# A hybrid SSM decoder step on one core: 16 modulation tiles moved into the SSD stage, sample states loaded by SyncE, mixer norms gathered

## Chip, cores and metric

One Trainium2 chip, one core. The metric is the device time of one execution in microseconds. Before the change the median of three runs is 2753.36 us (2751.09 to 2754.26).

## The reference

One decoder layer works on 256 prompt tokens and 8 sample tokens (one step for each of 8 sequences that carry states), D = 2048. A conditioning vector per sequence gives 6 x 2048 modulation values (`mod = silu(c) @ w_ada + b_ada`). The mixer has two halves, an SSD half (16 heads of 64) and a gated delta (GDN) half (8 heads of 128 x 128 state):

```
mod = silu(c) @ w_ada + b_ada
sh1, sc1, g1, sh2, sc2, g2 = split(mod, 6)
hm = rmsnorm(x, norm1_w) * (1 + sc1) + sh1
z, xbc, dt_raw, qkv, a_raw, b_raw, gate = split(hm @ w_in)
y = ssd_scan(conv(xbc), ...) ;  y = rmsnorm(y * silu(z), in 2 groups of 512)
o = gdn_scan(conv(qkv), ...) ;  o = rmsnorm(o, per head of 128) * silu(gate)
x = x + g1 * (concat(y, o) @ w_out)
hf = rmsnorm(x, norm2_w) * (1 + sc2) + sh2
x = x + g2 * peer(hf)        # product keys, top 16 of 128^2 experts
y_out = rmsnorm(x, final_norm_w)
```

For a sample token the GDN recurrence is one step: S is scaled by exp(g), k and q are multiplied with it, and beta k (v - S^T k)^T is added. The new states are outputs.

## The kernel before

Everything is float32; large products split weights and activations into a high and a low part and take three products of them. 264 columns are the 256 prompt tokens and 8 sample tokens. Weights come as tiles of 1 MB through a ring of four slots (`wring`), loaded by SyncE (SP) in one fixed order (lines 388 to 416): 32 w_ada tiles, 52 of w_in, 64 of w_ada (`N_ADA2`), 16 of w_out, 16 of w_q, then the experts. A slot is loaded again when `gemm_done` or `lo_ready` says that it has been used, so the order of the queue is the order of use.

Stages in order of time:

1. Modulation, first 32 tiles. One tile is 4 matmuls of 512 columns on TensorE (`ada_part`, L475); after four tiles ScalarE (ACT) copies bank 6 to `adasb` (L911, L1035, L1059) and four small matmuls turn it into columns of bank 7 (`ada_turn`), counted by the semaphore `ada_ps`. VectorE (DVE) later adds the bias into `mod`.
2. w_in with convolution and gates, to about 464 us.
3. SSD stage (TensorE L533 to L594), to about 525 us. GpSimd (POOL) writes decay rows to DRAM and loads them back broadcast to 128 partitions (`BR`, L1893, 4 MB). DVE builds decays, POOL the weighted x (L1902 to L1905), TensorE the first state (`h1_ps`), the final state (`hf_ps`), and y in two chunks (L574) and from the carried state (L586). No weight tile is used here; the next four w_ada tiles have landed before it.
4. GDN loop (L608), four passes of two heads, to about 726 us. Each pass has 12 w_ada tiles between the steps of its triangular inverse (`ada(i, j)`, L597). POOL updates the SSD states of two samples in each pass.
5. The tail, from `gdn_free` 5 (L690) to the first w_out tile (L718). TensorE's program is: `ada_rest(0)`; `norm(4)` twice (y, two groups of 4 tiles); the product for q.k; 64 small products of the sample states with k and q (`gst`, 128x128 by 2 columns), with `ada_rest(1)` in their middle; a transpose; four norms of one head and `ada_rest(2)`; four more and `ada_rest(3)`. POOL loads the eight pieces of `gst` (L1971, 512 KB each, in runs of 512 B) after its loop, and after the products scales both halves of them (L1977, recorded under L1876), which DVE waits for before `mixl` (L1579). A norm is: squares (ACT L877), a product with ones, root (ACT L886), reciprocal (DVE L1253), and scaling (DVE L1246). At its end ACT makes `mixh` and DVE `mixl`, the high and low parts of the concatenated y and o (L1079 to L1084).
6. w_out, 16 tiles. Per tile DVE makes the low part of the next tile's weights, adds the result to x, and adds k v^T to four sample states (L1611); POOL loads `gvb` for 16 states at a time (L1984) and stores the new states (L1989).
7. Norm, w_q, expert retrieval and experts, to the end.

Of the kernel before, what the change touches and what calls it, by code (L numbers as in the profile page):

```python
# [73 lines left out]
T_REST = T_ADA2 + 48  # L74
# [36 lines left out]
def build(nc, a, o):  # L111
    with ExitStack() as ctx:
# [132 lines left out]
        h1h, h1h_f = take_r(KT, T)  # L245
        mixh = view(zg_off, KT, T, of=F32R)
# [38 lines left out]
        vn, ksm, vsm = take(64), take(64), take(64)  # L285
        vrow = take(128, parts=64)
# [70 lines left out]
        def _(sp):  # L357
# [35 lines left out]
            four(a["w_out"], gemm_done, T_OUT)  # L393
            tiles(a["w_out"], lo_ready, L_OUT, N_OUT, first=1)
# [35 lines left out]
        def _(pe):  # L430
# [101 lines left out]

            pe.wait_ge(sem("zg_ready"), N_GATE + SLOTS)  # L533
            pe.wait_ge(sem("cv_ready"), 2 * CT + 8)
            for c in range(2):
                for j in range(8):
                    tr(ps[:, 2 * c + j // 4, (j % 4) * 128:(j % 4 + 1) * 128], cv[:, TX + j, c * CH:(c + 1) * CH]
                       ).then_inc(sem("xt_ps"), 1)
            pe.wait_ge(sem("cs_ready"), 1)
            for c in range(2):  # L540
                for g in range(2):
                    last = tr(ps[:, 7, (2 * c + g) * 128:(2 * c + g + 1) * 128], cv[:, TB + g, c * CH:(c + 1) * CH])
            last.then_inc(sem("bt_ps"), 1)
# [11 lines left out]
            last.then_inc(sem("h1_ps"), 1)  # L555

# [34 lines left out]

            pe.wait_ge(sem("y_evac"), 24)
# [4 lines left out]
            def ada(i, j):  # L597

                s, n = j % SLOTS, j // SLOTS
                pe.wait_ge(landed[s], i * 48 + (T_ADA2 // SLOTS * 16 + 16 * n + 16))  # L600
                if s == 0 and n:
                    ada_turn(i * 3 + (N_ADA1 // SLOTS + n), (n - 1) * (SLOTS * NC))
# [5 lines left out]
            with pe.Fori(0, 4) as i:  # L608
# [48 lines left out]
                ada_turn(i * 3 + (N_ADA1 // SLOTS + 3), 2 * SLOTS * NC)  # L657
# [26 lines left out]
            def ada_rest(g):  # L684
                for s in range(SLOTS):
                    pe.wait_ge(landed[s], 16 * (T_REST // SLOTS + g + 1))
                    ada_part(s)
                ada_turn((T_REST - T_ADA2 + N_ADA1) // SLOTS + g + 1, g * SLOTS * NC)

            pe.wait_ge(sem("gdn_free"), 5)  # L690
# [1399 lines left out]
```

## Time and profile before

| | us |
|---|---|
| median of three runs | 2753.36 |
| profiled execution | 2749.44 |
| its span, first to last instruction | 2747.9 |
| PE matmuls busy | 2487.0 (91%) |
| DVE busy | 1902.9 (69%) |
| ACT busy | 1003.3 (37%) |
| POOL busy | 484.8 (18%) |
| mean granted TensorE clock | 0.954 |

PE is TensorE's matmuls and PEld its weight loads, which overlap them. The profile is that of the profiled execution, 1.5 us shorter in its span than in its own device time. Busy shares are averages over stages with different limits. A clock of 1.00 is 2.4 GHz and 0.50 is 1.2 GHz. Most TensorE instructions carry the helper's line L437 (`mm`), and those of DVE L1240 (`tt`) or L1246 (`stt`), so they are told apart by time and shape. One float32 matmul is recorded as two instructions. In a timeline row of several instructions the duration runs from the first's start to the last's end.

### The profile page before, as it was taken

The page shows a single profiled execution, that of the slowest core. Times are in us where ns is not written, and L with a number is a line of the kernel's source. Part 1 is how long each engine was busy: PE and PEld are TensorE (multiplying, and loading weights), DVE is VectorE, ACT ScalarE, POOL GpSimd, SP SyncE. Part 2 cuts the span into 40 slices and gives each one's busy share as a digit, 9 for nine tenths or more (in the row PEclk, how much of TensorE's full clock was granted, in tenths as well). Part 3 has the DMA queues.
Part 4 walks back from the last instruction along what each step waited for, and adds up shares of the span by engine and source line. Part 5 has one row for each costly group of instructions (what it writes and reads, how often), then busy time and mean ns, then how long its engine had stood idle before and what let it go on. Part 6 is the DMA issues. An engine that isn't in the chain of part 4 may idle for free.

```text
span 2747.9 us, 54567 instructions
## 1 busy us (share of the span) xinstructions
PE 2487.0 (91%) x21637; PEld 2330.8 (85%) x21637; DVE 1902.9 (69%) x2496; ACT 1003.3 (37%) x1173; POOL 484.8 (18%) x221
## 2 busy tenths in 40 slices
PE   6489998687668799999899999999999999999998
PEld 2189997455448689899899999999999999999997
DVE  0377765534337678988999878778778778666666
ACT  1156686111113332144343333333334333333333
POOL 0000000455420110046333212112112121000000
PEclk8799999799869899999999999999999999999999
DMA  8545544387836733344344444454444444555553
GB/s 363 243 155 182 183 165 172 134 320 261 306 135 245 249 138 138 138 154 154 123 153 148 159 171 168 163 176 154 170 170 165 174 166 160 182 183 178 174 182 124
DMA packets 71422, 500.01 MB, mean 182 GB/s; under 512 B 8132, under 2 KB 8396, under 8 KB 14320
## 3 DMA queue, kind: packets, MB, share of 16 engines
q1 hardware_dynamic: 64368, 465.38, 46.7%
q0 software_dynamic: 6912, 32.50, 3.5%
q8 instruction: 117, 1.92, 0.3%
q14 instruction: 25, 0.20, 0.0%
HBM read 483.51 MB, written 14.35 MB: 181 GB/s over the span
## 4 chain that ended last, share of the span: by engine, by line
PE 81%; DVE 9%; DMA 4%; issue 4%; ACT 1%; POOL 1%; DVEq 0%; SPq 0%; ACTq 0%; POOLq 0%
PE ps L437 78%; DVE sb L1240 7%; DMA sb<-in_w_ada 3%; PE ps L475 2%; DVE sb L1246 1%; DVE sb L1243 1%; DMA sb<-rows_dram 0%; POOL sb L1876 0%; POOL sb L1971 0%; DMA sb<-in_state_gdn 0%; DVE sb L1253 0%; DMA out_gdn_state_s<-sb 0%; PE ps L574 0%; DVEq L1240 0%; ACT sb L936 0%
## 5 line engine op out<-in xcount | busy, mean ns | idle before, releaser
L437 PEld LDWEIGHTS ps<-sb,sb 128*128 128x128 f32 (+1 forms) x20680 | 2290.7, 176 | 285.3 <-issue 156.8
L437 PE MATMUL ps<-sb,sb 128*128 128x264 f32 (+5 forms) x20680 | 2352.2, 274 | 184.3 <-DVE sb L1240 94.2
L1240 DVE TENSOR_TENSOR sb<-sb,sb 128x264 fp32r<-128x264 f32 (+13 forms) x988 | 1321.7, 1372 | 370.3 <-ACT sb L936 250.7
L936 ACT CAST sb<-sb 128x2048 fp32r<-128x2048 f32 x327 | 624.8, 1911 | 566.7 <-PE ps L437 559.5
L1876 POOL TENSOR_TENSOR sb<-sb,sb 128x1056 bf16<-128x1056 bf16 (+3 forms) x158 | 439.6, 2789 | 1124.8 <-DVE sb L1240 1057.5
L1240 DVE TENSOR_TENSOR sb<-sb,ps 128x264 f32<-128x264 f32 (+2 forms) x577 | 248.6, 449 | 120.3 <-PE ps L437 100.0
L1205 ACT ACTIVATE sb<-ps 128x264 f32<-128x264 f32 x96 | 37.5, 391 | 359.0 <-PE ps L437 359.0
L475 PE MATMUL ps<-sb,sb 128*32 128x512 f32 x768 | 117.8, 710 | 34.1 <-DMA sb<-in_w_ada 22.8
L1240 DVE TENSOR_TENSOR sb<-ps,sb 128x256 f32<-128x256 f32 (+6 forms) x45 | 13.5, 327 | 159.2 <-PE ps L437 153.7
L1246 DVE SCALAR_TENSOR_TENSOR sb<-sb,sb,sb 128x288 f32<-128x288 f32 (+3 forms) x220 | 95.3, 462 | 21.8 <-DMA sb<-v_dram 3.9
L1122 ACT COPY sb<-ps 128x352 f32 (+1 forms) x96 | 82.4, 870 | 28.4 <-PE ps L437 28.3
L475 PEld LDWEIGHTS ps<-sb,sb 128*32 128x32 f32 x768 | 18.6, 119 | 83.7 <-DMA sb<-in_w_ada 53.1
L1886 POOL DMA_DIRECT2D rows_dram<-sb x1 | 0.7, 705 | 467.1 <-DVE sb L1364 467.1
L1150 ACT ACTIVATE sb<-ps 128x264 f32<-128x264 f32 x32 | 12.5, 390 | 153.3 <-PE ps L437 153.3
L1243 DVE TENSOR_SCALAR sb<-sb,sb 128x288 f32<-128x288 f32 (+2 forms) x69 | 24.8, 388 | 49.4 <-ACT sb L957 49.1
L1041 ACT COPY sb<-ps 128x512 f32<-128x512 f32 x24 | 14.1, 586 | 102.2 <-PE ps L437 102.2
L1246 DVE SCALAR_TENSOR_TENSOR sb<-ps,sb,sb 128x256 f32 (+1 forms) x24 | 10.2, 438 | 44.1 <-PE ps L437 44.1
L911 ACT COPY sb<-ps 128x512 f32<-128x512 f32 x8 | 4.7, 585 | 82.5 <-PE ps L475 82.5
L955 ACT COPY sb<-ps 128x256 f32<-128x256 f32 x36 | 13.5, 374 | 54.1 <-PE ps L437 54.1
L1348 DVE RECIPROCAL sb<-sb 128x264 f32<-128x264 f32 x16 | 28.7, 1797 | 5.8 <-ACT sb L980 5.8
L1253 DVE RECIPROCAL sb<-sb 128x264 f32<-128x264 f32 x13 | 23.4, 1799 | 11.5 <-ACT sb L886 11.4
L877 ACT ACTIVATE sb<-sb 128x264 f32<-128x264 f32 x64 | 24.7, 418 | 17.5 <-PE ps L437 10.9
(128 smaller groups left out, 500.3 us busy)
## 6 DMA issues: line engine op xcount, KB each, us to landing
sb<-in_peer_u SPq DMA_DIRECT2D x128, 1024.0 KB, 4.8
sb<-in_peer_v SPq DMA_DIRECT2D x128, 1024.0 KB, 4.7
sb<-in_w_ada SPq DMA_DIRECT2D x96, 1024.0 KB, 7.7
sb<-in_w_in SPq DMA_DIRECT2D x52, 1024.0 KB, 4.8
sb<-in_w_out SPq DMA_DIRECT2D x16, 1024.0 KB, 4.9
sb<-in_w_q SPq DMA_DIRECT2D x16, 1024.0 KB, 4.7
sb<-rows_dram POOLq DMA_DIRECT2D x1, 4096.0 KB, 11.9
sb<-in_state_ssd POOLq DMA_DIRECT2D x8, 512.0 KB, 5.5
```

Of the source, the lines that this page charges most:

```text
L437: return pe.matmul(out, l, r, start=start, stop=stop)
L475: last = pe.matmul(ps[32 * j:32 * j + 32, 6, :], sT[:, 4 * s + j, :], wring[:, s, :, :].rearrange("p (k c) n -> p k (c n)", k=4)[:, j, :], ...
L877: act.activation(sqb[:, n % 4, :], src, ACT.Square).then_inc(sem("sq_ready"), 1)
L936: act.copy(whi[:, slot % 2], wring[:, slot]).then_inc(sem("hi_ready"), 1)
L1122: act.copy(G[:, bass.ds(quarter, QE), bass.ds(t0, GT)].rearrange("p a t -> p t a"), ps[:, bank + b, 0:GT * QE].rearrange("p (t a) -> p t a ...
L1205: act.activation(craw[:, s % 2, :], ps[:, s % 2, 0:T], ACT.Gelu).then_inc(sem("gelu_done"), 1)
L1240: return dve.tensor_tensor(out, x, y, op)
L1243: return dve.tensor_scalar(out, x, s1, s2, op0, op1)
L1246: return dve.scalar_tensor_tensor(out=out, in0=x, scalar=s, in1=y, op0=op0, op1=op1)
L1253: link(dve.reciprocal(nrm[:, k % 2, :], nrm[:, k % 2, :]))
L1348: link(dve.reciprocal(r, r))
L1876: return pool.tensor_tensor(out, x, y, op)
```

## The change

- TensorE gets four groups of four w_ada tiles in the SSD stage: after the x transposes, after `h1_ps`, after `hf_ps`, and between the two y chunks. The loop of stage 4 then takes tiles 16 to 63 of the 64, and nothing is left for the tail. ACT copies these groups in `ada_early`; DVE adds `mod` of the 16 tiles ahead of the loop. Banks in the SSD stage are changed so that banks 6 and 7 are free.
- SyncE loads the sample states behind the first four w_out tiles: `gst1` after `gdn_free` 5, `gst0` after the last stores of `S2` and of the SSD states.
- The prompt columns of both mixers are normed together: 16 squares, 16 matmuls with a selecting weight of 32 columns into one bank of 32 rows, one root, one reciprocal of 32 rows; ten matmuls with a column of the identity spread each row to 128 partitions, and DVE scales from PSUM.
- The sample columns of o are normed apart, after the state products, 64 columns at once; `mixh` and `mixl` are made in three pieces.
- The states are scaled by DVE, four at a time, in the w_out loop, no longer by POOL.

The core of the diff:

```diff
-T_REST = T_ADA2 + 48
+N_SSD = 16
+T_GDN = T_ADA2 + N_SSD
...
             four(a["w_out"], gemm_done, T_OUT)
+            sp.wait_ge(sem("gdn_free"), 5)
+            for h in (4, 5, 6, 7):
+                sp.dma_start(gst1[:, 8 * (h % 4):8 * (h % 4) + 8, :], gdn_s_in[:, h]).then_inc(sem("ld_gst1"), 16)
+            for c in range(2):
+                sp.wait_ge(sem(f"sst_stored{c}"), 64)
+            sp.wait_ge(sem("s2_stored"), 64)
+            for h in range(4):
+                sp.dma_start(gst0[:, 8 * h:8 * h + 8, :], gdn_s_in[:, h]).then_inc(sem("ld_gst"), 16)
             tiles(a["w_out"], lo_ready, L_OUT, N_OUT, first=1)
...
+            def ada_tiles(g):
+                for s in range(SLOTS):
+                    pe.wait_ge(landed[s], T_ADA2 // SLOTS * 16 + 16 * g + 16)
+                    ada_part(s)
...
+            ada_tiles(0)
+            pe.wait_ge(sem("norm_sqrt"), 17)
             pe.wait_ge(sem("cs_ready"), 1)
...
             last.then_inc(sem("h1_ps"), 1)
+            ada_turn(A_SSD + 1, 0)
+            ada_tiles(1)
...
             last.then_inc(sem("hf_ps"), 1)
-            pe.wait_ge(sem("norm_sqrt"), 17)
+            ada_turn(A_SSD + 2, SLOTS * NC)
+            ada_tiles(2)
             pe.wait_ge(sem("h1_ready"), 1)
             for c in range(2):
                 pe.wait_ge(sem("m_ready"), c + 1)
                 if c == 1:
+                    ada_turn(A_SSD + 3, 2 * SLOTS * NC)
+                    ada_tiles(3)
                     pe.wait_ge(sem("y_evac"), 8)
...
+            ada_turn(A_SSD + 4, 3 * SLOTS * NC)
             pe.wait_ge(sem("y_evac"), 24)
...
             pe.wait_ge(sem("gdn_free"), 5)
-            ada_rest(0)
-            norm(4)
-            norm(4)
+            for j in range(2 * HG):
+                n = sq_n[0]
+                sq_n[0] += 1
+                row = j if j < HG else HG + (j - HG) // 4
+                pick = (row_o if j < HG else row_y)[:, 31 - row:63 - row]
+                pe.wait_ge(sem("sq_ready"), n + 1)
+                mm(ps[0:32, 4, 0:T], pick, sqb[:, n % 4, :], j == 0, j == 2 * HG - 1).then_inc(sem("sq_used"), 1)
...
+            pe.wait_ge(sem("ld_gst1"), 64)
+            state_products(range(32, 48))
+            pe.wait_ge(sem("rows_ready"), 1)
+            for j in range(2 + HG):
+                row = HG + j if j < 2 else j - 2
+                n = T if j < 2 else TP
+                bank, at = (5 + j, 0) if j < 2 else ((7, 0, 3, 4)[row // 2], row % 2 * TP)
+                mm(ps[:, bank, at:at + n], ident[0:32, row:row + 1].broadcast_to([32, P]), nrm[0:32, k17 % 2, 0:n]
+                   ).then_inc(sem("row_ps"), 1)
+            state_products(range(48, 64))
+            pe.wait_ge(sem("ld_gst"), 64)
+            state_products(range(32)).then_inc(sem("skq_ps"), 1)
             pe.wait_ge(sem("vns_ready"), 1)
-            for half in range(2):
-                for h in range(4):
-                    norm(1)
-                ada_rest(2 + half)
-            pe.wait_ge(sem("mixl_ready"), 2)
+            mm(ps[:, 6, 0:64], ones, sqb[:, n % 4, 0:64]).then_inc(sem("sq_used"), 1)
+            pe.wait_ge(sem("mixl_ready"), 3)
...
+            dve.reciprocal(rows, rows).then_inc(sem("rows_ready"), 1)
             for g in range(2):
-                r = inv_root()
+                dve.wait_ge(sem("row_ps"), g + 1)
                 for j in range(4):
                     t = 4 * g + j
+                    st.mark(stt(cv[:, TX + t, :], cv[:, TX + t, :], ynw[:, t:t + 1], ps[:, 5 + g, 0:T],
+                                ALU.mult, ALU.mult))
...
+            for h in range(HG):
+                dve.wait_ge(sem("row_ps"), h // 2 * 2 + 4)
+                v, at = cv[:, TQ + h, 0:TP], h % 2 * TP
+                st.mark(stt(v, v, onw[:, 0:1], ps[:, (7, 0, 3, 4)[h // 2], at:at + TP], ALU.mult, ALU.mult))
...
-            dve.wait_ge(sem("gst_scaled"), 2)
...
                         tt(xT[:, n, TP:T], xT[:, n, TP:T], gtmp[:, s, :], ALU.add).then_inc(sem("x1_done"), 1)
+                        four = gst[half][:, bass.ds(i * 16 + 4 * s, 4), :]
+                        link(tt(four, four, over(egc[:, bass.ds(i * 16 + (32 * half + 4 * s), 4)], 128, 2), ALU.mult))
...
-            for h in range(8):
-                pool.dma_start(gst[h // 4][:, 8 * (h % 4):8 * (h % 4) + 8, :], gdn_s_in[:, h]
-                               ).then_inc(sem("ld_gst"), 16)
-            pool.wait_ge(sem("skq_ps"), 1)
-            for j in range(2):
-                s4 = gst[j].rearrange("p (h b) v -> p h b v", b=TS)
-                tt(s4, s4, over(SR[:, 16 + 4 * j:20 + 4 * j, 0, :], 128, 3), ALU.mult).then_inc(sem("gst_scaled"), 1)
```

## Rows read from the trace of the kernel before

**Rows 1.** Stages: us, busy (count) per engine, PE clock, DMA share, GB/s
```profile
483.00:525.00 42.00, 18.92 (x136) 15.00 (x136) 26.74 (x47) 10.26 (x13) 10.20 (x5) 0.66 0.05 14
...
677.00:726.00 49.00, 42.17 (x320) 29.24 (x324) 17.91 (x33) 7.32 (x14) 29.31 (x20) 0.96 0.82 313
...
738.00:763.00 25.00, 0.00 (x0) 0.00 (x0) 4.26 (x8) 0.26 (x1) 4.40 (x5) 0.59 0.67 206
```

**Rows 2.** Timeline of the tail: start us, us, engine, instruction, count, [idle before]
```profile
725.88 5.21 PE L475 MATMUL ps<-sb,sb 128*32 128x512 f32 x32 [2.58 <-DVE sb L1246]
...
735.16 1.35 ACT L877 ACTIVATE sb<-sb 128x264 f32<-128x264 f32 x4
...
735.30 1.80 DVE L1253 RECIPROCAL sb<-sb 128x264 f32<-128x264 f32 x1 [5.60 <-ACT sb L886]
...
735.72 2.19 PE L437 MATMUL ps<-sb,sb 128*128 128x264 f32 x10 [0.97 <-ACT sb L877]
...
737.13 1.71 DVE L1246 SCALAR_TENSOR_TENSOR sb<-sb,sb,sb 128x264 f32<-128x264 f32 x4
...
748.39 2.64 POOL L1971 DMA_DIRECT2D sb<-in_state_gdn  x3 [15.94 <-issue]
...
763.72 13.78 PE L437 MATMUL ps<-sb,sb 128*128 128x2 f32 x64 [25.81 <-DMA sb<-in_state_gdn]
...
783.18 11.96 PE L437 MATMUL ps<-sb,sb 128*128 128x9 f32 x72 [0.71 <-ACT sb L1059]
...
795.23 14.01 POOL L1876 TENSOR_TENSOR sb<-sb,sb 128x4096 f32<-128x4096 f32 x2 [36.45 <-PE ps L437]
...
795.43 13.89 DVE L1240 TENSOR_TENSOR sb<-sb,sb 128x64 f32<-128x64 f32 x2
...
814.79 3.64 PE L475 MATMUL ps<-sb,sb 128*32 128x512 f32 x32
...
830.70 2.36 DVE L1240 TENSOR_TENSOR sb<-sb,sb 128x2112 f32<-128x2112 f32 x1
...
838.50 31.73 PE L437 MATMUL ps<-sb,sb 128*128 128x264 f32 x246 [5.06 <-DVE sb L1240]
```

**Rows 3.** Columns as rows 1, two microseconds within the products
```profile
789.00:791.00 2.00, 2.00 (x11) 2.00 (x11) 0.00 (x0) 0.00 (x0) 0.00 (x0) 0.50 1.01 426
```

**Rows 4.** DMA view, 748 to 757 us: rate in 40 slices; us to landing
```profile
GB/s 0 0 0 0 0 0 0 0 55 255 91 73 36 237 510 346 309 291 291 273 310 309 291 291 291 291 273 291 291 291 291 291 291 219 164 37 0 0 0 0
...
sb<-in_state_gdn POOLq DMA_DIRECT2D x3, 512.0 KB, 5.8
```

**Rows 5.** DMA view, first GDN pass, 525 to 576 us: rate in slices
```profile
GB/s 13 0 55 315 305 305 350 392 353 212 366 411 424 424 424 411 341 389 437 414 424 418 411 430 276 238 392 270 405 389 382 411 382 350 373 77 0 0 0 42
```

**Rows 6.** DMA view, 464 to 484 us: the broadcast, us to landing
```profile
sb<-rows_dram POOLq DMA_DIRECT2D x1, 4096.0 KB, 11.9
```

**Rows 7.** Timeline of the SSD stage, TensorE, columns as rows 2
```profile
485.90 3.75 PE L437 MATMUL ps<-sb,sb 128*128 128x512 f32 x4 [14.71 <-POOL sb L1876]
...
492.64 5.46 PE L437 MATMUL ps<-sb,sb 128*128 128x128 f32 x32 [2.98 <-POOL sb L1876]
...
498.03 1.97 PE L574 MATMUL ps<-sb,sb 128*64 128x128 f32 x32
...
509.31 3.68 PE L574 MATMUL ps<-sb,sb 128*64 128x128 f32 x32 [9.31 <-DVE sb L1240]
```

**Rows 8.** DMA view, 735 to 748 us, queues: packets, MB, share
```profile
q1 hardware_dynamic: 317, 2.22, 47.7%
q0 software_dynamic: 396, 1.43, 30.6%
```

**Rows 9.** DMA view, 473 to 476 us, within the broadcast
```profile
q0 software_dynamic: 32, 1.05, 83.4%
```

**Rows 10.** Groups by shape, 464 to 940 us: busy, mean ns, idle
```profile
L1240 DVE TENSOR_TENSOR sb<-sb,sb 128x512 f32<-128x512 f32 x12 | 12.4, 1029 | 3.5 <-ACT sb L1029 2.8 <-DVE sb L1240 0.2
```

**Rows 11.** Waits, 839 to 935 us: us in total, times, longest
```profile
DVE sb L1246 <- PE ps L437: 22.2, 15, 3.2
```

More of the change, by code:

```diff
@@ L245, in build @@
         h1h, h1h_f = take_r(KT, T)
+        row_y, row_o = take(64), take(64)
         mixh = view(zg_off, KT, T, of=F32R)
@@ L285, in build @@
         vn, ksm, vsm = take(64), take(64), take(64)
+        egc, bec = take(64), take(64)
         vrow = take(128, parts=64)
@@ L681, in _ @@
                 last.then_inc(sem("s_ps"), 1)
[L684 to L688, printed above, removed]
-            pe.wait_ge(sem("gdn_free"), 5)
-            ada_rest(0)
-            norm(4)
-            norm(4)
+            pe.wait_ge(sem("gdn_free"), 5)
+            for j in range(2 * HG):
[5 more added lines that the diff above has]
+                mm(ps[0:32, 4, 0:T], pick, sqb[:, n % 4, :], j == 0, j == 2 * HG - 1).then_inc(sem("sq_used"), 1)
+            k17 = norms[0]
+            norms[0] += 1
             pe.wait_ge(sem("qkp_ready"), 1)
@@ L1081, in _ @@
             act.wait_ge(sem("mix_ready"), 2)
-            act.copy(mixh[:, 8:16], cv[:, TQ:TQ + 8, :]).then_inc(sem("mixh_ready"), 1)
+            act.copy(mixh[:, 8:16, 0:TP], cv[:, TQ:TQ + 8, 0:TP]).then_inc(sem("mixh_ready"), 1)
+            high(0, T_OUT // SLOTS * 16 + 16, None)
+            act.wait_ge(sem("vrow_ps"), 1)
+            act.copy(vrow, ps[0:64, 5, 0:128]).then_inc(sem("vrow_ready"), 1)
+            act.wait_ge(sem("o_ready"), 1)
+            n, k18 = sq_n[0], norms[0]
+            sq_n[0] += 1
+            norms[0] += 1
+            act.wait_ge(sem("sq_used"), n - 3)
+            act.activation(sqb[:, n % 4, 0:64].rearrange("p (h b) -> p h b", b=TS), cv[:, TQ:TQ + 8, TP:T], ACT.Square
+                           ).then_inc(sem("sq_ready"), 1)
+            act.wait_ge(sem("sq_used"), n + 1)
+            act.activation(nrm[:, k18 % 2, 0:64], ps[:, 6, 0:64], ACT.Sqrt, scale=1.0 / P, bias=epsc[:, 0:1]
+                           ).then_inc(sem("norm_sqrt"), 1)
+            act.wait_ge(sem("mix_ready"), 3)
+            act.copy(mixh[:, 8:16, TP:T], cv[:, TQ:TQ + 8, TP:T]).then_inc(sem("mixh_ready"), 1)
             def high_next(i, s, t0):
@@ L1434, in _ @@
             dve.sem_inc(sem("ysm_ready"), 1)
+            dve.wait_ge(sem("ada_ps"), A_GDN)
+            link(tt(mod[:, 32:48, :], ps[:, 7, 0:16 * NC].rearrange("p (n c) -> p n c", c=NC),
+                    over(bada[:, 32:48], NC, 2), ALU.add))
             dve.wait_ge(sem("norm_free"), 17)
```

143 lines of the change are left out of this document (78 added, 65 removed).

## The prediction

> **What bounds the kernel now.** I read the busy time by stage first [rows 1]. The gated-delta loop (GDN) keeps TensorE (PE) busy 42 us of 49. Between that loop and w_out it does not: for 25 us it does nothing at all (738 to 763). The SSD stage is thin as well: behind the broadcast of the decay rows PE works 18.9 of 42 us while the DMAs move 14 GB/s. These two places are what the change touches. Then the timeline of the tail [rows 2]: the GDN loop lets PE go at 725.88 (call it G), and the first w_out matmul starts at 838.50, G+112.6. Between them lie, one after another, 16 modulation tiles in four groups; sample states that come so late that the products start at 763.72; 64 head products around one of the groups; a sample update on DVE, two instructions that are held for 13.89 us while POOL scales the states; eight norms with a reciprocal of 1.80 us each; two copies and two subtractions of 128x2112. Then the granted clock [rows 3], the DMAs [rows 4 to 6] and the SSD stage [rows 7], whose PE waits 14.71 us for the broadcast.
>
> **The tail, part by part.** All times are from G.
> Norm sums: 16 matmuls of 264 columns. At full clock one costs 0.44 us (10 matmul instructions in 2.19 us, two per matmul) [rows 2]. PE comes out of the loop slow: its first 32 modulation matmuls took 5.21 us, against 3.64 for 32 at 814.79 [rows 2]. That is 1.6 us lost, so some 3.3 us at half clock, and 3.3 + 12.2 x 0.44 = 8.7 us. The squares on ACT, 0.34 each (1.35 for 4) [rows 2], are faster than that and hide beside PE; without that cover they would be 16 x 0.34 = 5.4. One root (0.5), then one reciprocal, still 1.80 though it has 32 rows, since the row at 735.30 pays for its 264 columns: rows ready at G+11.2.
> States: SyncE issues gst1's four loads at G and gst0's about 3 us later, when the last gdn_p store has landed; the w_out tiles that stand before them in its queue land during the last GDN pass. POOL's loads, alone, moved some 291 GB/s [rows 4]: 2.1 MB in 7.2 us, seen about 2 us later, gst1 at G+9.7 and all at G+17.5. POOL's issue stall of 15.94 us [rows 2] goes with the queue. No row shows SyncE loading pieces of 512 B. From below, the 424 GB/s of weight tiles [rows 5]: all at G+12. From above, one behind another at the 5.8 us landing of POOL's loads: gst1 at G+23, all at G+46. I take POOL's rate, the same pieces on the same DMAs.
> Products: 16 of them fill the wait for the rows, 32 instructions x 0.107 = 3.4 us, G+13.3. Ten row matmuls of 256 to 264 columns, 4.4 us, G+17.7. 48 products are left, 96 instructions. Before, 64 instructions took 13.78 us, 0.215 each, half clock; the 72 at 783.18 took 11.96, which is a mixture, and PE stood at 0.50 from 789 to 791 though it was busy without a gap [rows 2, 3]. If x of the 72 ran at 0.107 and the rest at 0.215, 11.96 us gives x = 33, some 3.6 us. I count 4 us at full clock (37 instructions) and 59 instructions at 0.215, 12.7 us: G+34.4.
> Here the Trainium skill says otherwise. "TensorE: Matmul & The Clock Gate", What's actually happening, has the gate set by how busy PE has been, so that unbroken products should hold the full clock. By that rule they would end at G+28. The trace does not agree: busy 2.00 of 2.00 us, clock 0.50 [rows 3].
> DVE: 8 y and 8 o scalings at 0.43 to 0.49 us (1.71 for 4), the gate and one half of mixl at 2.36 each [rows 2] end at G+26.8, and ACT's copies and first high part at G+28.3: both inside the products, which are their cover.
> Behind the products: six small updates 1.6, mixl of the prompt 2.3, reciprocal of 64 columns 0.45 (an estimate, 1.80 x 64/264), scaling, gate, copy and subtraction 1.3: 5.7 us. The first w_out matmul at G+40.1. **Tail 112.6 to 40.1: -72.5.** Late next is PE itself.
>
> **What it costs elsewhere.** SSD stage. A group of four tiles is 3.6 to 5.2 us of PE [rows 2], plus a turn of 1 to 1.9. Group 0 (landed long before) lies in the 14.71 us wait: nothing. But it frees its slots from 470 on, so 4.2 MB of weights start beside the 4.2 MB broadcast that lands 11.9 us after its issue [rows 6]. Where two queues shared, that with 8 KB packets had 47.7% and that with 4 KB packets 30.6% [rows 8], so shares go by packet. The broadcast's packets are 32 KB [rows 9]; an 8 KB packet between any two of them adds a quarter of its 10 us: +3 (ends: 0, weights wait behind it; +10, even bytes). Group 1 sits between the first-state and the final-state product: h1 ends at 492.7, turn and tiles take until 498.5, where the operands are there at 495.6. Group 2 waits for its tiles: slots free from 495.4, four tiles at 424 GB/s [rows 5] take 9.9 us and 2 to be seen, 507.5. PE reaches the y product at 508.7, before at 498.03 [rows 7]: +10.7. Group 3 is hidden: its last tile lands at about 517 and is done at 518.3, and the next operand comes 11.3 us after the y product (509.31 - 498.03), at 520. With PE busy before it, the block that took 3.68 us for the instructions that took 1.97 at 498.03 [rows 7] runs partly at full clock, and the next too: -1.5. One addition of mod is new before the loop: 0.3. **SSD +9.5**, ends +4 and +20 (no landing hidden).
> GDN loop: 12 tiles a pass as before, the first four landed before it starts: 0.
> w_out: DVE gets 16 scalings of 128x512, taken at 0.7 us; the nearest group of that size has 1.03 in the mean, POOL beside it [rows 10]. DVE waits 22.2 us for PE in 15 tiles, 1.5 each [rows 11], so this is hidden; without the cover 11 to 16 us. Only the last one lies on the path, before the last state store: +0.8.
> **Sum: -72.5 + 9.5 + 0.8 = -62.** The profiled execution took 2749.44 (span 2747.9 and 1.5 around it), so 2687. The median of the three runs is 2753.36, 3.9 above it: I say 2691.
>
> **Rivals.**
> 1. Even sharing. The weights take half of the DMAs from the broadcast: it lands at +10 instead of +3, SSD +16, in sum 2697. The packets of 8 and 32 KB speak against [rows 8, 9]. The Trainium skill, "DMA: Bandwidth & Descriptors", SWDGE vs HWDGE vs iDMA, gives a packet as preferably at most 4096 B and as the boundary at which an engine changes queues; by that rule the shares would be even. Chance 0.15.
> 2. The clock holds in the products, as norm and row matmuls stand around them: -6.3, 2685. The 13.78 us at half clock speak against [rows 2]. 0.12.
> 3. Late states. With half of the upper bound's lateness gst0 lands at G+32, the 32 products on it take 13.8 us, w_out starts at G+51.5: 2702. At the bound, G+46: 2716. POOL's issue stall can have been its own queue's, which speaks against. 0.13.
> 4. The modulation part does nothing: only the 26 us of waiting for states and POOL's 14 go, and SSD's +10 stays: 2723. Rows of 5.21 and 3.64 us for its groups in the chain speak against [rows 2]. 0.03.
> 5. Slower. DVE bounds w_out, since each scaling, which is on DVE now, is held as the two updates were (6.9 us each) [rows 2]. 16 x (6.9 - 1.5) = 86, in sum +24: 2777. It decides from 1.5 + 62/16 = 5.4 us a scaling. For it: both read two SBUF operands. Against: POOL only issues DMAs in this stretch. 0.02.
>
> **How the numbers follow.** My case has 0.55, the rivals 0.15, 0.12, 0.13, 0.03 and 0.02. The range takes in its bounds (SSD +4 and +20), rivals 1 and 2 whole and most of 3: 2676 to 2712. A measurement of this kernel can tell about 0.2%, 5.5 us, from no change. Faster by more: 0.96. Within: 0.02. Slower by more: 0.02.
>
> **What would show it.** Right: no POOL tensor_tensor of 4096 and no held update; products at clock 1.0 and then 0.50; first w_out matmul 40 us after the GDN loop; the loop starting 9.5 us later, rows_dram landing in 15 us; PE waiting for in_w_ada once in the SSD stage, before the y product; DVE still waiting for PE in w_out. Wrong: PE waiting for in_state_gdn past G+18; rows_dram over 20 us; a GDN loop more than 2 us longer; PE waiting for DVE in w_out.

## The result, and the profile after

The changed kernel takes 2732.9 us (median of 7 executions, 2720.5 to 2738.4), the kernel before, on the same chip, 2751.7. The ratio is 0.9927, 95% interval 0.9905 to 0.9949: faster by some 20 us, where the forecast was 62 and its range ended at 2712. The profiled execution of the changed kernel took 2735.1 us with a span of 2733.5.

To see where the other 42 us went, each kernel was profiled four times (the first two profiles and runs e1, e5, e12 to e15 below); before: the first, e5, e12, e14; after: the first, e1, e13, e15. The stages, cut at TensorE's (PE's) first matmul in each, means of four in us:

| stage | before | after | difference | forecast |
|---|---|---|---|---|
| start to first GDN matmul (SSD stage) | 525.5 | 549.6 | +24.1 | +9.5 |
| GDN loop | 202.1 (200.8 to 204.4) | 209.4 (207.6 to 211.4) | +7.3 | 0 |
| tail, loop to first w_out matmul | 112.3 | 51.4 | -60.9 | -72.5 |
| w_out to w_q | 129.6 | 131.6 | +2.0 | +0.8 |
| w_q to the end | 1780.8 | 1788.2 | +7.4 | 0 |
| span | 2750.4 | 2730.3 | -20.1 | -62 |

Every stage has a part in the miss, even the one behind w_q, whose code the change does not touch. The same stretches of the changed kernel as [rows 1], columns as there: the SSD stage from 485 us, the last GDN pass, the tail.

```profile
485.00:551.00 66.00, 36.03 (x267) 22.53 (x268) 27.88 (x50) 12.83 (x18) 10.34 (x5) 0.71 0.68 268
709.00:761.00 52.00, 44.19 (x315) 31.16 (x314) 19.33 (x30) 8.29 (x18) 29.35 (x20) 0.92 0.81 293
761.00:811.00 50.00, 43.75 (x187) 35.77 (x188) 22.53 (x40) 14.62 (x22) 1.91 (x3) 0.61 0.37 96
```

PE is now busy in the tail 43.8 us of 50, but at a mean clock of 0.61: it is the bound there, and a slow one. In the SSD stage the DMAs, which moved 14 GB/s [rows 1], move 268.

**The SSD stage.** Timeline of the changed kernel, PE, columns as rows 2; L489 are the modulation tiles, the x8 matmuls of L451 with 128x9 the turns, L601 the y products of the two chunks, L614 the product behind them. The last line is the broadcast in the list of DMA issues (KB, us to landing), which answers to [rows 6].

```profile
495.33 4.63 PE L451 MATMUL ps<-sb,sb 128*128 128x512 f32 x12 [18.37 <-POOL sb L1954]
499.89 3.64 PE L489 MATMUL ps<-sb,sb 128*32 128x512 f32 x32
...
508.02 1.92 PE L489 MATMUL ps<-sb,sb 128*32 128x512 f32 x16
510.88 1.06 PE L489 MATMUL ps<-sb,sb 128*32 128x512 f32 x8 [0.94 <-DMA sb<-in_w_ada]
514.89 1.06 PE L489 MATMUL ps<-sb,sb 128*32 128x512 f32 x8 [2.94 <-DMA sb<-in_w_ada]
515.88 3.42 PE L601 MATMUL ps<-sb,sb 128*64 128x128 f32 x32
528.45 1.88 PE L451 MATMUL ps<-sb,sb 128*128 128x9 f32 x8 [9.14 <-DVE sb L1295]
530.25 5.11 PE L489 MATMUL ps<-sb,sb 128*32 128x512 f32 x32
535.29 1.97 PE L601 MATMUL ps<-sb,sb 128*64 128x128 f32 x32
541.91 3.68 PE L614 MATMUL ps<-sb,sb 128*64 128x128 f32 x32 [4.65 <-DVE sb L1295]
...
550.24 3.70 PE L451 MATMUL ps<-sb,sb 128*128 128x128 f32 x16 [1.97 <-ACT sb L1082]
```
```profile
sb<-rows_dram POOLq DMA_DIRECT2D x1, 4096.0 KB, 18.2
```

Read it by its gaps. The broadcast lands 18.2 us after its issue instead of 11.9. Groups 1 and 2 stand in front of the first y product (515.88; before 498.03 [rows 7], and this execution ran 2.0 us late even ahead of the stage, so +15.8), group 2 with two waits for its tiles. Then PE waits 9.14 us for VectorE (DVE), and only behind that wait come the turn and the tiles of group 3: 6.8 us between the operand's arrival at 528.45 and its use at 535.29. From the first to the second y product it is 19.4 us, before 11.3.

Executions reach this stage at different times: PE's first transposes in it (x8, 128*32) start between 462.25 and 467.50 us in the eight profiles. Counted from there, the GDN loop starts after 61.2 us before (61.0 to 61.6) and after 85.0 us in the changed kernel (84.1 to 85.6), +23.8.

**The tail.** The loop lets PE go at 761.15 (G). Timeline, columns as rows 2:

```profile
761.12 4.94 SPq L402 DMA_DIRECT2D sb<-in_state_gdn  x4
761.15 9.36 PE L451 MATMUL ps<-sb,sb 128*32 128x264 f32 x34 [2.58 <-DVE sb L1301]
...
770.76 1.79 DVE L1618 RECIPROCAL sb<-sb 32x264 f32<-32x264 f32 x1 [5.35 <-ACT sb L1118]
...
771.59 32.81 PE L451 MATMUL ps<-sb,sb 128*128 128x2 f32 x148 [1.08 <-DMA sb<-in_state_gdn]
783.76 20.55 PEld L451 LDWEIGHTS ps<-sb,sb 128*128 128x128 f32 x96 [0.65 <-issue]
784.89 4.56 DVE L1295 TENSOR_TENSOR sb<-sb,sb 128x2048 f32<-128x2048 f32 x2 [0.15 <-DVE sb L1301]
...
804.44 0.23 DVE L1295 TENSOR_TENSOR sb<-ps,sb 128x64 f32<-128x64 f32 x1 [14.98 <-PE ps L451]
...
810.53 1.68 PE L451 MATMUL ps<-sb,sb 128*128 128x264 f32 x6 [3.38 <-DVE sb L1295]
```

PEld are the weight loads; the x96 are those of the last 48 products. The window 776 to 805 us (columns as rows 1):

```profile
776.00:805.00 29.00, 28.40 (x115) 26.14 (x113) 11.81 (x21) 5.65 (x3) 0.00 (x0) 0.50 0.06 14
```

One norm of the prompt's columns with one reciprocal, the first states after 10.4 us, no GpSimd (POOL) instruction and no held update: the tail does what the diff says. But PE, busy 28.4 of 29 us, stands at half clock in all of it. DVE, done with the scalings and the gate at 789.5, waits 14.98 us for the last product.

**The code behind w_q.** PE in the first big expert loop, about 102 us a pass, columns as rows 2; first the kernel before, then the changed one:

```profile
1644.83 99.68 PE L437 MATMUL ps<-sb,sb 128*128 128x264 f32 x966 [1.83 <-issue]
```
```profile
1621.81 2.32 PE L451 MATMUL ps<-sb,sb 128*128 128x264 f32 x17 [1.54 <-issue]
1625.42 97.59 PE L451 MATMUL ps<-sb,sb 128*128 128x264 f32 x949 [1.30 <-issue]
```

"Issue" is time in which PE waited for nothing that the profile shows. The matmuls are the same 966; before there is one such stall a pass, after it a second one 17 matmul instructions later. In all there are 9 (14.8 us) before and 16 (22.7 us) after. In the means of the four profiles it is 14.6 and 22.0 us: the stalls account for the whole +7.4 of this stretch.

### The profile page after: what moved, and what is told of

The parts are those of the page before. It is cut to its first block, busy times and chain, and to the rows that moved or that the text cites. A ratio compares the mean times of both kernels' runs of the same rounds, so it can differ in the third digit from the quotient of the medians.

```text
span 2733.5 us, 54636 instructions
## 1 busy us (share of the span) xinstructions
PE 2506.5 (92%) x21659; PEld 2344.1 (86%) x21659; DVE 1887.9 (69%) x2513; ACT 1001.3 (37%) x1167; POOL 464.2 (17%) x211
## 3 DMA queue, kind: packets, MB, share of 16 engines
q8 instruction: 118, 1.93, 0.3%
## 4 chain that ended last, share of the span: by engine, by line
PE 81%; DVE 8%; DMA 6%; issue 4%; ACT 1%; DVEq 0%; SPq 0%; POOL 0%; ACTq 0%; POOLq 0%
PE ps L451 78%; DVE sb L1295 6%; DMA sb<-in_w_ada 4%; PE ps L489 2%; DVE sb L1301 1%; DMA sb<-rows_dram 1%; DVE sb L1298 1%; DMA sb<-in_state_gdn 0%; PE ps L454 0%; DVE sb L1308 0%; PE ps L601 0%; DMA out_gdn_state_s<-sb 0%; ACT sb L981 0%; PE ps L614 0%; DVE sb L1831 0%
## 5 line engine op out<-in xcount | busy, mean ns | idle before, releaser
L451 PEld LDWEIGHTS ps<-sb,sb 128*128 128x128 f32 (+2 forms) x20702 | 2304.8, 177 | 283.5 <-issue 156.4
L451 PE MATMUL ps<-sb,sb 128*128 128x264 f32 (+5 forms) x20702 | 2371.6, 275 | 177.2 <-DVE sb L1295 99.4
L1954 POOL TENSOR_TENSOR sb<-sb,sb 128x1056 bf16<-128x1056 bf16 (+2 forms) x156 | 425.9, 2735 | 1113.9 <-DVE sb L1295 1067.9
L489 PE MATMUL ps<-sb,sb 128*32 128x512 f32 x768 | 117.7, 707 | 31.5 <-DMA sb<-in_w_ada 22.8
L1301 DVE SCALAR_TENSOR_TENSOR sb<-sb,sb,sb 128x288 f32<-128x288 f32 (+4 forms) x205 | 88.2, 459 | 22.6 <-DMA sb<-v_dram 4.1
L1177 ACT COPY sb<-ps 128x352 f32 (+1 forms) x96 | 82.2, 869 | 28.4 <-PE ps L451 28.3
L489 PEld LDWEIGHTS ps<-sb,sb 128*32 128x32 f32 x768 | 18.1, 117 | 79.9 <-DMA sb<-in_w_ada 54.8
L1205 ACT ACTIVATE sb<-ps 128x264 f32<-128x264 f32 x32 | 12.5, 391 | 152.9 <-PE ps L451 152.9
L1407 DVE RECIPROCAL sb<-sb 128x264 f32<-128x264 f32 x16 | 28.7, 1797 | 5.8 <-ACT sb L1025 5.8
L1301 DVE SCALAR_TENSOR_TENSOR sb<-sb,sb,ps 128x128 f32<-128x128 f32 (+2 forms) x40 | 13.6, 397 | 27.8 <-PE ps L601 22.3
## 6 DMA issues: line engine op xcount, KB each, us to landing
sb<-rows_dram POOLq DMA_DIRECT2D x1, 4096.0 KB, 18.2
```

What stands on the lines that cost most here:

```text
L451: return pe.matmul(out, l, r, start=start, stop=stop)
L489: last = pe.matmul(ps[32 * j:32 * j + 32, 6, :], sT[:, 4 * s + j, :], wring[:, s, :, :].rearrange("p (k c) n -> p k (c n)", k=4)[:, j, :], ...
L1177: act.copy(G[:, bass.ds(quarter, QE), bass.ds(t0, GT)].rearrange("p a t -> p t a"), ps[:, bank + b, 0:GT * QE].rearrange("p (t a) -> p t a ...
L1301: return dve.scalar_tensor_tensor(out=out, in0=x, scalar=s, in1=y, op0=op0, op1=op1)
L1407: link(dve.reciprocal(r, r))
L1954: return pool.tensor_tensor(out, x, y, op)
```

## The experiments

Ratios are to the kernel before, with 95% intervals; a total in us is a median. Time differences between stages are read from the profiles.

### e1: the changed kernel again
No edit.

> The changed kernel once more, for the spread of its stages. If the GDN loop's 210.9 us (+10.2 against before) and the two issue stalls in every pass of the first big expert loop (1.5 and 1.3 us, where before has one of 1.8) belong to the change, both come back here within 1 us and 0.2 us: loop 210 to 212 us, w_q to the end +9 to +10 us against the profile of before. If they are noise of one execution, the loop comes out between 201 and 208 us, or the second stall is missing. Ratio to before 0.993 as measured.

Measured: 2731.3 us, ratio 0.9899 (0.9875 to 0.9923). Loop 211.35, two stalls a pass, w_q to the end 1786.2, against 1779.9 in the profile of before: +6.3, less than the +9 expected. All four surprises of the first profile came back. On this chip the kernel before took 2756.1 us, so the gain is 25 us here, at the upper end of what the first comparison allows.

### e2: the same code, 24 instructions further on
```diff
+            for _ in range(24):
+                mm(ps[0:32, 7, 480:482], ident[:, 0:32], ident[:, 0:2])
             pe.wait_ge(sem("mixl_ready"), 3)
             with pe.Fori(0, N_OUT // SLOTS) as i:
```


> The changed kernel with 24 tiny matmuls (32x2) ahead of w_out, which only move TensorE's later code on by 24 instructions. Theory (instruction fetch): in every pass of the first big expert loop TensorE stalls on issue twice, the second time 17 matmuls behind the loop's start, because that is where a block of fetched code ends; with the code 24 instructions further the second stall (1.3 us, 8 passes) is gone, and from w_q to the end it takes 8 to 10 us less, against some 2 us for the 24 matmuls. Total -6 to -8 us against the changed kernel. Rival (the +9.8 us behind w_q come from something else, such as DMA or a loop's wait): two stalls a pass as before, total +2 us.

Measured: 2723.3 us, 8.0 less than e1 on the same chip (6.3 in the means of six executions); ratio 0.9882 (0.9859 to 0.9906). In the big expert loop:

```profile
1714.66 99.56 PE L451 MATMUL ps<-sb,sb 128*128 128x264 f32 x966 [1.61 <-issue]
```

The second stall is gone (9 in all, 15.7 us), and w_q to the end takes 1781.9. More instructions made the kernel faster: what hurt was where the loop's code lies. The edit of e6 has its tiny matmuls write to another bank than this one (1 instead of 7), and so do those of e8 and e10.

### e3: group 3 ahead of the wait
```diff
             for c in range(2):
-                pe.wait_ge(sem("m_ready"), c + 1)
                 if c == 1:
                     ada_turn(A_SSD + 3, 2 * SLOTS * NC)
                     ada_tiles(3)
+                pe.wait_ge(sem("m_ready"), c + 1)
+                if c == 1:
                     pe.wait_ge(sem("y_evac"), 8)
```


> The changed kernel with the turn and the tiles of modulation group 3 ahead of TensorE's wait for the second chunk's operand instead of behind it. Theory: behind the wait they lie on the path with 1.9 + 5.1 us, ahead of it they fill the 9 us in which TensorE waits for VectorE, so that the second chunk's products start 5 to 7 us earlier after the first's (19.4 us apart now, 11 to 13 before) and the total falls by 5 to 7 us. Rival (VectorE, which evacuates y behind it, or the w_ada tiles' landing, ends last anyway): the second product earlier but the GDN loop's start the same, total -1 to 0 us.

Measured: 2721.4 us, 9.9 less than e1; ratio 0.9873 (0.9851 to 0.9896). PE, columns as rows 2:

```profile
516.72 3.30 PE L602 MATMUL ps<-sb,sb 128*64 128x128 f32 x32
...
520.94 1.92 PE L489 MATMUL ps<-sb,sb 128*32 128x512 f32 x16
523.58 1.07 PE L489 MATMUL ps<-sb,sb 128*32 128x512 f32 x8 [0.71 <-DMA sb<-in_w_ada]
526.06 1.73 PE L489 MATMUL ps<-sb,sb 128*32 128x512 f32 x8 [1.41 <-DMA sb<-in_w_ada]
529.17 3.68 PE L602 MATMUL ps<-sb,sb 128*64 128x128 f32 x32 [1.39 <-DVE sb L1296]
```

12.5 us between the products instead of 20.6 in e1, and the loop starts 4.7 us earlier than there. This is the theory's mechanism. The cover is nearly used up: PE waits twice for group 3's tiles, the last of which is there at 526.06, and only 1.39 us are left to wait for DVE. Of the 8.1 us won between the products only 4.7 are left at the loop's start: the first product came 1.0 later in this execution, and 2.4 go behind the second, whose matmuls take 3.68 us here and 1.97 in e1. The rest of the 9.9 is not: here the loop took 203.5 us, the least of all kernels with 16 moved tiles, at a mean clock of 0.96.

### e4: weights held back until the broadcast has landed
```diff
+            sp.wait_ge(sem("ld_br"), 16)
+            sp.wait_ge(sem("ld_sr"), 16)
             tiles(a["w_ada"], gemm_done, T_ADA2, N_ADA2, t0=N_ADA1, first=1)
```


> The changed kernel with SyncE waiting for the landing of the two broadcasts (rows, samples) before it reloads the w_ada slots. Theory (the broadcast shares the DMA engines with the reloaded weight tiles): the broadcast lands again 12 us after its issue instead of 18.2, VectorE goes on 5 to 7 us earlier, the first y product starts 3 to 5 us earlier, total -3 to -5 us. Rival (the weight tiles then come later and groups 1 and 2 wait for them in front of the y product): broadcast 12 us, but the y product no earlier or later by up to 4 us; total 0 to +4 us. Third way (POOL's own queue makes the broadcast slow, not the sharing): landing stays at 17 to 19 us, total 0 to +6 us.

Measured: 2727.0 us, 4.2 less than e1 in the medians, but 0.9 in the means of six, and the ratio of 0.9899 (0.9873 to 0.9925) is that of e1: a gain in the total is not shown. What the profile shows is the stage. The broadcast:

```profile
sb<-rows_dram POOLq DMA_DIRECT2D x1, 4096.0 KB, 12.9
```

First y product at 512.49 (e1 515.67), loop start 3.7 us earlier. So it is the reloaded weight tiles that cost the broadcast some 5 us, and in this stage holding them costs less than it saves: the groups then wait 3.9 us for tiles, about as long as in e1 (4.1).

### e5, e12, e14: the kernel before again; e13, e15: the changed kernel again


> The kernel before once more, for its spread. If the changed kernel's longer GDN loop (203 to 211 us in five profiles of it and its variants) is a matter of the granted clock in the loop's passes (0.905 to 0.97) and not of the change, this loop too can leave 200.75 us, towards 205 or more with a lower clock; if it belongs to the change, it stays at 200 to 202 us with a clock of 0.96. One issue stall a pass in the first big expert loop, w_q to the end 1778 to 1782 us.

> The kernel before again, for the GDN loop. If the changed kernel's longer loop is the spread of executions, this loop, too, lies anywhere between 200 and 212 us (so far 200.8, 201.5 and, with 11 tiny matmuls behind the loop, 207.3); if the change lengthens it, 200 to 208.

> The changed kernel again. If its loop is longer by itself: 206 to 212 us (so far 210.9 and 211.4); if it is spread: anywhere between 200 and 212.

> As the kernel before in the first run of this call: a loop of 200 to 212 us if it is spread, of 200 to 208 us if the change lengthens it.

> As the changed kernel in the second run of this call: a loop of 206 to 212 us if the change lengthens it, anywhere between 200 and 212 if it is spread.

Measured loops: before 201.5, 204.4 and 202.0; changed 207.6 and 207.9. With the two first profiles and e1 that is 200.8 to 204.4 against 207.6 to 211.4: the spread is real, about 4 us in either kernel, and does not bridge the 7.3 between the means. On one chip (e12 to e15) the difference is 4.6. The other experiments blur it further: all ten profiles with 16 moved tiles have loops of 203.5 to 212.4 us (mean 208.6), and the five with before's loop, e6 below among them, 200.8 to 207.3 (mean 203.2). The loop's window in one profile of each (before in e12, changed in e15), columns as rows 1:

```profile
524.00:729.00 205.00, 172.96 (x1268) 120.77 (x1272) 82.21 (x136) 32.71 (x62) 119.99 (x83) 0.93 0.80 299
```
```profile
550.00:758.00 208.00, 174.00 (x1266) 120.75 (x1266) 79.49 (x134) 33.97 (x66) 119.97 (x83) 0.93 0.80 295
```

At the same clock of 0.93 the changed loop is still some 3 us longer; at 0.96 (e3) likewise 203.5 against 200.8. The other part goes with the clock: 0.91 in both profiles of 211 us. In the means of four PE is busy 4.4 us longer with as many instructions (175.8 against 171.5 us), and it waits 3.4 us longer for modulation tiles (2.2 to 6.2 us in a loop, before 1.1 to 2.0). But e6, whose loop is before's, has 6.2 us of that wait too. What lowers the clock in some passes, and why more often after the change, I did not settle.

### e6: the kernel before, 11 instructions further on
The edit of e2 with 11 matmuls, in the kernel before, ahead of its w_out loop.

> The kernel before with 11 tiny matmuls (32x2) ahead of w_out: the expert loop's code is then as far on as the change puts it. Theory (where the code lies decides the second stall): two issue stalls a pass, the second about 17 matmuls behind the loop's start, 0.5 to 1.5 us each, w_q to the end 1785 to 1790 us instead of 1780, total +5 to +9 us against before. Rival (the second stall needs the change itself): one stall a pass and 0 to +1 us.

Measured: 2769.3 us, ratio 1.0057 (1.0039 to 1.0075), 15 us slower. The theory's sign and its mark, a second stall 13 matmul instructions behind the start:

```profile
1648.66 1.86 PE L437 MATMUL ps<-sb,sb 128*128 128x264 f32 x13 [1.66 <-issue]
1651.97 98.10 PE L437 MATMUL ps<-sb,sb 128*128 128x264 f32 x953 [1.46 <-issue]
```

Eleven matmuls of 32x2 cost the kernel before as much as three quarters of what the change as a whole gains. The size is above what I expected: w_q to the end is 14.3 us longer, of which the stalls (16 instead of 9, 25.5 us instead of 13.4 to 15.4) explain 10 to 12; the rest stays open. Apart from that the GDN loop took 207.3 us, 5 more than the mean, though neither the loop nor anything ahead of it was edited. One of before's loops can thus be as long as the shortest of the changed kernel's.

### e7: the modulation move alone
The kernel before with the 16 tiles in the SSD stage and without its four groups in the tail; norms, the states' loads and their scaling as before.

> The kernel before with the modulation move alone: 16 tiles in the SSD stage as in the changed kernel, the tail without them, but its ten norms, the states' loads by GpSimd and their scaling there as before. Theory: the SSD stage is 23 us longer as in the changed kernel, the loop 0 to 10 us; the tail loses the 64 tile products of 3.6 to 5.0 us a group and the turns behind them, 25 to 35 us of 112.6 us; total -10 to +5 us against before, so that the change's gain is nearly all in the root and the loads. Rival (my prediction's view that the move is worth its place): SSD stage +10, total -15 to -25 us.

Measured: 2770.1 us, ratio 1.0056 (1.004 to 1.0073): the move by itself makes the kernel 16 us slower, slower than my theory allowed. The stages: start to loop 545.8, loop 212.4, tail 98.7 (112.3 before). Here is why the tail gains only 13.6 us from 16 tiles less, columns as rows 2:

```profile
786.64 27.44 PE L441 MATMUL ps<-sb,sb 128*128 128x2 f32 x128 [16.05 <-DMA sb<-in_state_gdn]
814.17 14.01 POOL L1884 TENSOR_TENSOR sb<-sb,sb 128x4096 f32<-128x4096 f32 x2 [32.37 <-PE ps L441]
814.38 13.89 DVE L1248 TENSOR_TENSOR sb<-sb,sb 128x64 f32<-128x64 f32 x2
```

PE waits 16 us for the states, the products take 27.4 at half clock, and POOL's scaling still holds DVE. The groups had stood in waits that remain without them. The other 47.3 us of the tail's gain (98.7 to 51.4) belong to the one root, the loads by SyncE and the scaling that left POOL; these were not taken apart, and a kernel that has them without the move was not run.

### e8: three edits together
e2, e3 and e4 in one kernel.

> The changed kernel with the three edits together: group 3 ahead of the wait, SyncE holding the weight tiles until the broadcasts have landed, and 24 tiny matmuls that move the expert loop's code. Theory: their effects add up, -4 for group 3, -4 for the held tiles where the first product starts earlier, -7 for the stall: 2714 to 2720 us beside a changed kernel of 2731, ratio to before 0.985 to 0.988. Rival (the tiles held back are late for group 3 as well, now that it comes early): the second product not earlier than in the changed kernel, total -7 to -9 us only.

Measured: 2713.2 us, ratio 0.9849 (0.9831 to 0.9866), 18.1 below e1; the three apart gave 8.0 + 9.9 + 4.2 = 22.1. In the means it is 15.6 and 6.3 + 7.7 + 0.9 = 14.9, so that within the spread they add up. In the stage itself they do: counted from the first transposes, the loop starts 8.4 us earlier than in e1, where e3 had 5.5 and e4 2.7. The loop took 209.6 us, not e3's 203.5.

### e9: wide matmuls among the products
```diff
                 for j in pairs:
+                    if j % 4 == 0:
+                        mm(ps[:, 1, 64:448], ident, gst1[:, 0:3, :])
                     last = mm(ps[:, 2, 2 * j:2 * j + 2], gst[j // 32][:, j % 32, :], kq[:, j, :])
```


> The changed kernel with one full-width matmul (128x384, into columns nobody reads) ahead of every fourth product of the tail, 16 in all. Theory: the clock falls behind 775 us because products with 2 columns keep TensorE's queue busy but its array idle; with wide matmuls among them the granted clock stays at or near 1.00 through the products, a product costs 0.22 instead of 0.43 us, and they end 3 to 8 us earlier against the tail's start although the 16 fillers cost 5 us themselves. Rival (the clock falls for the waits ahead of the products, whatever runs in them): clock 0.50 as before, the products end 5 to 10 us later.

Measured: 2742.1 us, ratio 0.9957 (0.9936 to 0.9977), slower than the changed kernel. The clock around the start of the products, and deep in them (columns as rows 1), then the fillers by shape:

```profile
766.00:768.00 2.00, 1.64 (x11) 1.41 (x12) 0.00 (x0) 0.00 (x0) 0.00 (x0) 1.00 1.20 289
768.00:770.00 2.00, 2.00 (x9) 1.56 (x8) 0.00 (x0) 0.00 (x0) 0.00 (x0) 0.57 1.21 290
...
810.00:814.00 4.00, 4.00 (x14) 2.97 (x13) 0.00 (x0) 0.00 (x0) 0.00 (x0) 0.50 0.00 0
```
```profile
L451 PE MATMUL ps<-sb,sb 128*128 128x384 f32 x32 | 24.9, 881 | 3.1 <-DMA sb<-in_state_gdn 3.1
```

The theory fell: the fillers, at 0.88 us an instruction, had 24.9 us of the stretch of 53.8 and the clock stayed at 0.50. The tail became 72.0 us, 20.6 longer than the mean. The total hides a part of that: the fillers move the loop's code too, the second stall is gone (9 stalls, 14.3 us), and w_q to the end takes 1781.1 us. That the 2-column products alone are to blame is not shown; that wide work in 46% of the time does not cure it is.

### e10: the move spread over four waits
12 tiles in the SSD stage (group 0 in the broadcast's wait, 1 in the wait for the second chunk's operand, 2 behind its products), the last group at G; the w_out tiles queued behind the states; e2's and e4's edits.
```diff
-N_SSD = 16
+N_SSD = 12
...
             for c in range(2):
+                if c == 1:
+                    ada_turn(A_SSD + 1, 0)
+                    ada_tiles(1)
                 pe.wait_ge(sem("m_ready"), c + 1)
...
+            ada_turn(A_SSD + 2, SLOTS * NC)
+            ada_tiles(2)
             pe.wait_ge(sem("ce_ready"), 1)
...
             pe.wait_ge(sem("gdn_free"), 5)
+            for s in range(SLOTS):
+                pe.wait_ge(landed[s], 16 * (T_REST // SLOTS + 1))
+                ada_part(s)
```


> The move spread by where TensorE waits: 12 tiles in the SSD stage instead of 16 (group 0 in the broadcast's wait, group 1 in the wait for the second chunk's operand, group 2 behind the second chunk's products), the last group at the tail's start, SyncE holding the tiles until the broadcasts have landed and loading the states ahead of w_out's tiles, and the 24 tiny matmuls. Theory: the first y product no longer stands behind two groups and starts at about 500 us instead of 515, the GDN loop at 527 to 532 instead of 550 (525 before); the tail is 0 to 4 us longer than the changed kernel's 49 to 52; total 2698 to 2706 us. Rival (the groups' late tiles move the waits: group 2 waits behind the second product): loop's start at 535 to 540, total 2705 to 2715.

Measured: **2700.8 us, ratio 0.9817 (0.9797 to 0.9836)**, 52 below the kernel before and 30 below e1, the fastest of all. PE, columns as rows 2:

```profile
460.08 2.33 PE L454 MATMUL ps<-sb,sb 128*32 128x128 f32 x8 [3.91 <-DVE sb L1430]
...
496.79 1.97 PE L601 MATMUL ps<-sb,sb 128*64 128x128 f32 x32
...
499.67 3.64 PE L492 MATMUL ps<-sb,sb 128*32 128x512 f32 x32
508.06 3.68 PE L601 MATMUL ps<-sb,sb 128*64 128x128 f32 x32 [4.75 <-DVE sb L1305]
...
513.48 5.05 PE L492 MATMUL ps<-sb,sb 128*32 128x512 f32 x32
518.45 1.97 PE L616 MATMUL ps<-sb,sb 128*64 128x128 f32 x32
...
524.68 3.78 PE L454 MATMUL ps<-sb,sb 128*128 128x128 f32 x16 [2.68 <-DVE sb L1305]
```

The loop starts at 524.68, as early as before (525.13), but this execution reached the stage 4 us sooner, at 460.08 instead of 464.11. Counted from there, twelve tiles cost the stage 3.4 us (64.6 against 61.2; 64.7 in e11), where 16 cost 23.8 in the change and 15.4 in e8. The first y product comes 36.7 us after the transposes, before 33.9, and PE still waits 4.75 us for DVE behind group 1. The fourth group costs the tail some 2 us (53.2; the changed kernel 49.4 to 53.5). Of the 30 us against e1 a part belongs to the held tiles and the moved code; e8 has these and group 3's early place, and e10 is 12 us below it.

### e11: e10 with the fillers


> The spread version with the 16 full-width fillers among the tail's products. If the fillers keep the clock, 3 to 8 us below the spread version; if not, 5 to 8 us above it.

Measured: 2720.2 us, ratio 0.9887 (0.9869 to 0.9905), 19.4 above e10. Same verdict as e9, and a worse size than the 5 to 8 that I had given it: at half clock a filler costs twice what I had counted.

## Why the prediction was wrong

The sign was right, and so were most of the tail's steps. The size was not: forecast -62, measured -20.1 in the means. The 42 us between them are SSD +14.6, tail +11.6, code behind w_q +7.4, GDN loop +7.3, w_out +1.2. Two steps of the sum failed most: the place of group 3, wrong in its mechanism, and the count of instructions at each clock in the tail, the largest single term. Two stages that I had put at nothing took another 14.7 us.

**"Group 3 is hidden: its last tile lands at about 517 and is done at 518.3."** This mechanism was wrong. I set the tiles' landing against the operand's arrival and did not look at which side of the wait the group stands. In the diff it is behind the wait for m_ready, and PE takes its instructions in order: the turn starts at 528.45, when the operand is there, though there was room for it in the 9.14 us of waiting. That is 6.8 us on the path; with the group ahead of the wait (e3) its turn and tiles run before the operand comes, and the loop starts 4.7 earlier. The landing at 517 was wrong too: in e3 the last tile is there at 526.06.

**"Shares go by packet ... +3."** The broadcast landed 6.3 us later. The rule of sharing held. In the DMA view from 480 to 488 us, while both queues ran (packets, MB, share of the DMAs; q0 is POOL's, with the broadcast, q1 SyncE's, with the weight tiles), they took turns packet by packet, and by its packets of 32 KB the broadcast had four parts in five of the bytes:

```profile
q0 software_dynamic: 81, 2.65, 77.2%
q1 hardware_dynamic: 83, 0.68, 20.1%
```

What my price had not in it was a late start. From 474 to 478 us, the first 4 us after the broadcast's issue, the weight tiles had the DMAs nearly alone:

```profile
q1 hardware_dynamic: 144, 1.10, 93.8%
q0 software_dynamic: 6, 0.13, 7.6%
```

The first packet of 32 KB started 3.9 us after the issue (3.9 to 4.2 in the changed kernel's four profiles), before 1.3; that is 2.5 us. The 128 packets then took 12.4 us to start instead of 9.0, +3.4, which is my +3. Why the first one comes late no run shows. So rival 1's even bytes fell, although the landing lies between its +10 and my +3. The Trainium skill, "DMA: Bandwidth & Descriptors", SWDGE vs HWDGE vs iDMA, takes a packet as preferably at most 4096 B and as what an engine switches on. The trace agrees with the switching, 81 packets against 83; with packets of 32 and 8 KB it did not make the bytes even. With the later landing and the waits of 3.9 us for group 2's tiles the first y product came 15.8 us later instead of 10.7. I had worked out the right mechanism for groups 1 and 2 and sized it short.

**"I count 4 us at full clock (37 instructions) and 59 instructions at 0.215: G+34.4."** The count of instructions at each clock was the mis-sized term, 8.9 us of the tail's 11.6. Full clock did last about 4 us, but from the first product at 771.59, so that the first 32 instructions used it up. The ten row matmuls went at half clock, 0.87 us each instead of 0.44 (+4.3), and all 96 instructions of the 48 products at 0.215 (+3.9). They ended at G+43.3, 8.9 late; the rest of that is mostly the first states, 0.7 later than forecast. This profile's tail is 49.4 us; the mean of the four, 51.4 (49.4 to 53.5), adds another 2.0 to the miss. Rival 2, the clock that holds, went the other way altogether. The Trainium skill's page "TensorE: Matmul & The Clock Gate", What's actually happening, ties the clock to how busy PE is; PE was busy 28.40 of 29.00 us at 0.50, so this tail does not bear it out, as [rows 3] had said.

Right in the tail: rows ready at G+11.4 (forecast 11.2), first states G+10.4 (9.7), all of them at G+17.5 (17.5) at about 290 GB/s from SyncE's queue as from POOL's, DVE's scalings and gate inside the products (at 789.5, G+28.3; forecast 26.8), and 6.1 us behind the products (5.7). Rival 3 (late states) fell, and rival 5 (scalings that hold w_out) fell: 16 of them took 11.1 us, 0.69 each, and DVE still waited for PE:

```profile
L1295 DVE TENSOR_TENSOR sb<-sb,sb x16 | 11.1, 692 | 0.6
L1301 DVE SCALAR_TENSOR_TENSOR sb<-ps,sb,sb 128x256 f32 x16 | 7.7, 484 | 12.1 <-PE ps L451 11.7 <-issue 0.3
```

The first line, from the groups by shape of DVE from 811 to 940 us, is the scalings; the second shows the wait at 11.7 us, where it was 22.2 [rows 11]. The cover had room. The stretch to w_q is 2.0 us longer, 1.2 more than I gave it.

**"GDN loop: ... 0."** It is 7.3 us longer in the mean. I listed "a GDN loop more than 2 us longer" as what would prove me wrong and gave it no price. Part goes with a lower clock in the passes. Longer waits for modulation tiles are in it as well, 3.4 us in the means, but before's loop had them once too (e6). What brings on either stays open.

**What no term covered.** Where an unchanged loop's code lies was in none of my cases. It cost 7.4 us in the mean (e2 gives 6.3 of them back, and the stalls' 22.0 us against 14.6 are all of it), more than a tenth of my sum. Nothing in the trace of before could have priced it, though its stalls on issue, one a pass, were there to be seen.

**Rival 4** (the modulation part does nothing) had 0.03, and 2723 us is nearest of all to the result. That nearness is luck: it had 40 us for the tail, where 60.9 were gained, and 10 for the SSD stage, where 24.1 were lost. But it was right about the move's worth: its 16 tiles take 13.6 us out of the tail (e7), and put more than that into the stages ahead. The rows of 5.21 and 3.64 us that I had held against it show what a group takes, not what its going would free.

## What to carry to other kernels

Before you call moved work hidden, write down the order in which its engine issues: work behind a wait starts when the wait ends, whenever its data has come, and the same group ahead of the wait can run inside it (e3). Move work into several waits, each no shorter than the piece it takes, rather than all of it ahead of one product (e10 against e8, which shares the held tiles and the moved code: 12 us). And when a program is lengthened ahead of a long loop, compare the stalls on issue inside that loop in both profiles: a few instructions more can be worth as much as the edit under study.

## What the runs showed of the hardware that I had not expected

- PE's stalls on issue at a loop's start depend on where the code lies. 11 small matmuls ahead of it add a second stall of about 1.5 us a pass (e6, w_q to the end +14.3 us); 24 more in the changed kernel take it away (e2, 1788.2 in the mean to 1781.9), and so do the fillers of e9 (1781.1). The page shows a DMA queue named instruction with 118 packets and 1.93 MB, 16 KB each; that the stall is a wait for such a packet was only argued.
- The granted clock fell to 0.50 some 2 to 4 us after the 2-column products began, with PE busy throughout, and stayed there for the 29 us of them and the row matmuls. It did so in e10, too, where no idle time stood ahead of them, and with 384-column matmuls making up 46% of the stretch (e9). In w_out, with 264 columns, it was at 0.50 from 811 to 815 us and at 0.80 from 815 to 819.
- A broadcast of 4.2 MB in 32 KB packets, with 2.6 MB of weight tiles in 8 KB packets beside it, lands after 18.2 us instead of 11.9; with the weights held back, after 12.9. While both run, the queues take turns by packets (81 and 83 in 8 us); the broadcast's first packet comes 3.9 us after its issue instead of 1.3.
- State loads in pieces of 512 B go as fast from SyncE's queue (8 loads of 0.5 MB, about 290 GB/s while they run) as they did from POOL's [rows 4].
